# First expert's second row half gathered in three pieces: between the first half's turning and its products, and behind two weight units

## The reference

```python
e_idx = g_star[:, None].astype(jnp.int32) * EXPERTS_PER_GROUP + top_i.astype(jnp.int32)
y = grouped_experts(x, e_idx, w.astype(x.dtype), w_gate, w_up, w_down)

def expert_block(args):
    xblk, e = args
    return (jax.nn.silu(xblk @ w_gate[e]) * (xblk @ w_up[e])) @ w_down[e]
```

## Time and profile before

| | |
|---|---|
| median of 3 runs | 1435.9 us (1434.64 to 1437.3) |
| the profiled execution | 1436.35 us, span 1434.4 us |
| busy: PE, DVE, ACT, POOL | 87%, 30%, 15%, 3% of the span |
| mean granted TensorE clock | 0.947 |
| moved by DMA | 503.63 MB, 351 GB/s over the span |

### The profile page before, as it was taken

How to read it: one execution, slowest core, us unless ns; L and a number is a source line. 1 busy time by engine, 2 the same in 40 slices (tenths; PEclk the granted TensorE clock), 3 DMA queues, 4 the chain that set the end, 5 groups by cost and what they waited for, 6 DMA issues and landing times.

```text
span 1434.4 us, 21171 instructions
## 1 busy us (share of the span) xinstructions
PE 1242.1 (87%) x8998; PEld 675.9 (47%) x8998; DVE 433.2 (30%) x863; ACT 217.4 (15%) x462; POOL 45.4 (3%) x33
## 2 busy tenths in 40 slices
PE   9999999999999998997877778796787787777887
PEld 8888888888788862331222232132232122213223
DVE  4322127674211143322311321231222231132142
ACT  3111232322000043110101111011011010101101
POOL 0000003140000001000000000000000000000000
PEclk9999999999999999998989998899999898999899
DMA  9975443669399359999999999999999999999997
GB/s 342 348 227 183 140 133 121 206 206 340 88 349 413 121 182 427 417 425 435 427 433 432 430 433 431 431 431 431 431 432 432 430 432 432 432 432 430 433 426 317
DMA packets 101202, 503.63 MB, mean 351 GB/s; under 512 B 9294, under 2 KB 79638, under 8 KB 86182
## 3 DMA queue, kind: packets, MB, share of 16 engines
q1 hardware_dynamic: 89346, 494.86, 85.0%
q10 hardware_dynamic: 11812, 8.14, 1.8%
HBM read 496.42 MB, written 6.59 MB: 351 GB/s over the span
## 4 chain that ended last, share of the span: by engine, by line
PE 53%; DMA 44%; DVE 2%; ACT 1%; issue 0%; DVEq 0%; ACTq 0%; SPq 0%
PE bank L735 31%; DMA ring<-in_w_gate 16%; DMA ring<-in_w_up 15%; DMA ring<-in_w_down 12%; PE bank L1023 9%; PE bank L1058 3%; PE bank L958 2%; PE bank L1076 1%; DVE xa L1913 1%; PE bank L1073 1%; DMA xa<-in_x_prompt 1%; PE bank L746 0%; PE bank L826 0%; PE bank L776 0%; PE bank L1084 0%
## 5 line engine op out<-in xcount | busy, mean ns | idle before, releaser
L1023 PE MATMUL bank<-ring,bc 128*32 128x512 f32 x2040 | 272.4, 669 | 113.7 <-DMA ring<-in_w_gate 61.9
L735 PE MATMUL bank<-bc,ring 128*128 128x264 f32 x1536 | 350.8, 387 | 1.3 <-ACT cat L1261 1.3
L735 PEld LDWEIGHTS bank<-bc,ring 128*128 128x128 f32 x1536 | 288.2, 190 | 51.5 <-issue 2.3
L1023 PEld LDWEIGHTS bank<-ring,bc 128*32 128x32 f32 x2040 | 63.7, 118 | 288.2 <-issue 146.5
L1913 DVE TENSOR_TENSOR xa<-xa,bank 128x512 f32<-128x512 f32 x128 | 79.3, 682 | 153.0 <-PE bank L1076 146.6
L735 PE MATMUL bank<-cat,ring 128*128 128x264 f32 x512 | 114.9, 387 | 0.0
L735 PEld LDWEIGHTS bank<-cat,ring 128*128 128x128 f32 x512 | 97.0, 190 | 17.7 <-issue 1.3
L1927 DVE COPY bc<-bank 128x512 f32<-128x512 f32 x32 | 22.1, 691 | 234.6 <-PE bank L1023 234.6
L1058 PE MATMUL bank<-ring,cat 128*32 128x512 f32 x480 | 67.2, 684 | 22.4 <-DMA ring<-in_w_down 22.4
L958 PE MATMUL bank<-cat,bc 128*32 128x512 f32 x512 | 61.3, 597 | 13.5 <-DVE xa L1913 13.5
L1487 ACT ACTIVATE bc<-bank 128x512 f32<-128x512 f32 x32 | 19.1, 597 | 289.6 <-PE bank L1023 289.6
(11 more groups left out here) (300 smaller groups left out, 1023.5 us busy)
## 6 DMA issues: line engine op xcount, KB each, us to landing
ring<-in_w_gate SPq DMA_DIRECT2D x27, 4096.0 KB, 31.8
ring<-in_w_up SPq DMA_DIRECT2D x27, 4096.0 KB, 31.6
ring<-in_w_down SPq DMA_DIRECT2D x26, 4096.0 KB, 32.7
ring<-in_w_in SPq DMA_DIRECT2D x23, 2048.0 KB, 15.3
ring<-in_w_up SPq DMA_DIRECT2D x10, 2048.0 KB, 12.9
ring<-in_w_gate SPq DMA_DIRECT2D x9, 2048.0 KB, 15.4
ring<-in_w_down SPq DMA_DIRECT2D x9, 2048.0 KB, 16.1
ring<-in_w_out SPq DMA_DIRECT2D x8, 2048.0 KB, 16.5
```

The costliest lines, as they stand in the source:

```text
L735: m = pe.matmul(bank[n % 3][:, 0:T], w[:, k, (i % TPU) * P:(i % TPU + 1) * P], src[:, k, :], start=n_k == 0, stop=n_k == KT - 1)
L1023: m = pe.matmul(bank[b][c * C:(c + 1) * C, :], xeT[j % 2][:, k, :], wx, start=i == 0 and x < 4, stop=i == 1 and x >= 4, skip_group_check=True)
```

## The change

`first_rows` takes a list of row tiles, and the turning becomes a function `turn_first`. The first half's rows are gathered as before. Of the second half, the part of prompt tile 0 comes next, then the turning of the first half, then the part of prompt tile 1. The sample part and the turning of the second half stand behind the first expert's g0 and u0. No other engine's code changes.

```diff
-            def first_rows(half):
+            def first_rows(half, ts):
 
-                for t in range(TT):
+                for t in ts:
...
-                m.then_inc(first_gathered, 1)
+                if TT - 1 in ts:
+                    m.then_inc(first_gathered, 1)
 
             keep_busy(6)
-            first_rows(0)
-            first_rows(1)
-            for half in range(2):
+            def turn_first(half):
+
                 pe.wait_ge(first_copied, half + 1)
                 for m_ in (2 * half, 2 * half + 1):
                     m = pe.transpose(bank[(5, 7)[half]][:, m_ * P:(m_ + 1) * P], xrow[:, m_ * P:(m_ + 1) * P], ident)
                 m.then_inc(xe_T, 1)
+
+            first_rows(0, range(TT))
+            first_rows(1, (0,))
+            turn_first(0)
+            first_rows(1, (1,))
...
                         unit_products(j, "g", 0)
                         unit_products(j, "u", 0)
+                        if first:
+                            first_rows(1, (2,))
+                            turn_first(1)
                         pe.wait_ge(xe_ready, 2 * e + 2)
                         unit_products(j, "g", 1)
                         unit_products(j, "u", 1)
```

## The result

The changed kernel takes 1440.47 us in the median of 20 runs (1438.66 to 1444.83), the kernel before 1436.35; the ratio is 1.0027 with a 95% interval of 1.0020 to 1.0034, that is 3.9 us (2.9 to 4.9) slower. One execution of the kernel before took 1607.73 us, and the ratio, which compares fast runs, leaves it out. A second comparison, on another occasion, gives 1.0024 (1.0015 to 1.0033). The profiled execution took 1439.9 us with a span of 1438.1.

The account below looks back on a forecast made before the run. The end was taken to hang on unit 19's issue at 577.06 us, set by TensorE's chain. Terms -1.0 + 1.0 + 1.1 + 1.33 gave +2.4 us, so 1438.3 us, with an 8-in-10 range of 1436.4 to 1440.3.

Parts of the forecast that it names:

- What bounds the kernel: Weight stream last stands still until unit 19's issue at 577.06 us, set by TensorE's chain; the end follows from that.
- Part one: Start of g0: g0 and u0 start 1.0 us sooner, and units 10 and 11 are issued 1.0 us sooner.
- Part two: Second half behind u0: waits of some 0.4 us for its copy and 0.5 for its gain; TensorE alone loses 1.1 us.
- Part three: ScalarE's queue behind the copy, 3.98 us later: fold waits another 1.33 us for the gate copy, starting 2.4 us later.
- the sum: Whole kernel: -1.0 (g0 sooner) + 1.0 (moved work) + 1.1 (copy and gain waits) + 1.33 (fold wait) = +2.4 us.
- Part four: From the fold to unit 19: the shift passes one to one, so unit 19 is issued at 579.5 us.
- the clock rival: TensorE's clock falls at the fold's 1.33 us idle time, adding 1.8: sum 4.2 us, 1440.1 us; 10% chance.
- how the numbers follow: Odds with 0.2% (2.9 us) resolvable: forecast 70%, own range 1437.3 to 1439.5; slower 0.31, same 0.66, faster 0.03.
- The fold does not wait: Rival at the first fold: ScalarE catches up, leaving +1.1 us, 1437.0 us; 8% chance.
- the shift is absorbed: Rival between 544 and 577 us, or at the end: a wait has reserve, nothing reaches 577.06; 1435.9 us, 7%.
- The sooner start is what counts: Rival at 577 us: the stream runs through, so the 1.0 us won at 533 is kept; 1434.9 us, 5%.

Follow-up runs that it names:

- a_defer: Changed kernel with ScalarE's eight sample-row copies moved from ahead of the gate-product copy to behind the first expert's gate matrix; 1438.78 us, ratio 1.0011.
- b_defer: Kernel before with ScalarE's eight sample-row copies moved behind the first expert's gate matrix, as a control; 1436.6 us, ratio 0.9998.
- c_turn: Changed kernel with the sample part back ahead of g0 and only the second half's turning moved, between g0 and u0; 1436.9 us, ratio 1.0000.
- f2_fill: Changed kernel with one 512-column filler product ahead of the first fold and one fewer small product before the gathering; 1440.32 us, ratio 1.0040.
- g2_fill: Kernel before with two 512-column filler products in TensorE's wait near 568 us and two fewer small ones before the gathering; 1436.26 us, ratio 0.9994.
- d_early: Kernel before with two of ScalarE's four prompt tile 0 copies moved ahead of its copy of the first down products; 1434.9 us, ratio 0.9987.
- after_again: The changed kernel once more, unchanged, for a second trace; 1441.6 us, ratio 1.0024.
- h_best: Kernel before with the second half turned between g0 and u0 and ScalarE's prompt tile 0 copies split (c_turn and d_early together); 1435.01 us, ratio 0.9987.
- f_fill: Changed kernel with four small filler products on TensorE ahead of the first fold; 1450.27 us, ratio 1.0098 in four runs.
- g_fill: Kernel before with six small filler products in TensorE's wait near 568 us; 1446.17 us, ratio 1.0068 in five runs.

## Why the prediction was right, and where it was short

**What bounds the kernel** was right, and more exactly than I had claimed. Over nine traces (of the kernel before, the changed one, a_defer, b_defer, c_turn and f2_fill) the span is unit 19's issue plus 857.3 to 857.6 us, while unit 19's issue itself moves over 5 us. g2_fill's 856.4 goes with a tail at full clock. d_early shows the limit of the statement: it holds as long as the stream runs dry.

**Part one** was right: g0 starts 0.99 us sooner behind the gathering (forecast 1.0), and so does unit 10's issue.

**Part two** was 0.1 short. TensorE's own loss is 15.32 - 14.09 = 1.23 us in a_defer, where I had 1.1; the two pauses are 0.50 and 0.52, and the sample part moves at full price (0.63 us in both kernels).

**Part three** was right. ScalarE's copy of the second half slipped by 4.1 us against the gathering (3.98 forecast), its queue kept its 8.3 us, and the fold waited 1.19 us (forecast 1.33). a_defer takes that wait away and gets 1.3 us back, b_defer shows that the copies cost nothing by themselves. The measured structural loss is 2.50 us, the sum said 2.43.

**Part four** was right for the structure: fold to unit 19 is 35.04 us in both kernels. Its words "I take the shift one to one" left out that this stretch has two lengths. Where the clock falls behind the wait near 568 us it takes 36.3 to 36.7.

**The size** was short: 2.4 against 3.9 (2.9 to 4.9), and the slower side of 0.2%, to which I had given three tenths. A difference of 3.9 lies outside of the forecast's own range (1.4 to 3.6 us over 1435.9) and only inside the wide one (0.5 to 4.4), and the median itself, 1440.47, is 0.2 above the top of that, 1440.3; that the wide range held is in part luck. The nearest figure was the clock rival's 4.2, but the one profiled execution of the changed kernel has no fall where that rival put it.

The step that failed is "how the numbers follow": I treated the clock as a rival that is there or not, at 10%, with one place. The traces show it falling now and then at 520 us (in the changed kernel and d_early), near 573 us (in both kernels) and at the fold (in the changed kernel alone), 1.0 to 1.6 us each time. The one profiled execution of the kernel before, on which the sum rests, had none of these. In the three traces of the changed kernel there are one, two and two, in the two of the kernel before none and one. One more fall in the median would be enough for the missing 1.4 us; five traces can't show that it is there. That the changed kernel has more of them because of its idle time at the fold was seen in one trace of three, and f2_fill, whose long runs stay though this idle time is filled, speaks against it as the only source. What makes the changed kernel's long runs stays open.

The 1.8 us in that rival's sum are the 5.34 us of the earlier trace rows, at a granted clock of 0.50, less half of the 7.07 us of the earlier trace rows: one fall at 644 us in the kernel before, where the falls between 515 and 600 us cost 1.0 to 1.6. Against the rival the prediction sets an idle time of 1.81 us that left the clock at 1.00. The trace of after_again shows a fall behind 1.23 us all the same, and the other two of the changed kernel show none behind 1.19 and 1.21.

**The other rivals.** "The fold does not wait" and "the shift is absorbed" are out by the traces. "The sooner start is what counts" is out for this kernel (c_turn), and comes true in the trace of h_best, once unit 19 is early enough: 0.4 us, which the medians do not resolve.

## What to carry to other kernels

Before a wait is moved later on one engine, read what is queued behind it there: here a copy of 0.38 us slipped by 4 us, and took 8 us of unrelated work with it past its reserve of 1.6. Work that hands over from engine to engine (copy, turning, gain) belongs ahead of a unit that can hide each step, not all behind one: here that was two pauses of 0.50 and 0.52 us, and in c_turn none. And in a stream-bound kernel look for the last moment at which the stream runs dry: what moved that moment (66 GB/s at 577 us in the kernel before) moved the end here, up to the point where the stream no longer ran dry, as in d_early (377 GB/s).

## What the runs showed of the hardware that I had not expected

A few more instructions were a cliff here. Four products more in TensorE's straight part raised the packets of instructions from 33 to 88 (0.54 to 1.44 MB, 16 KB each) and cost 11 us in a loop behind them; a filler of like length at an unchanged number of instructions (f2_fill) left the packets at 33 and the end at 857.6 us behind unit 19. The packets and the waits in the loop come together: six waits without a releaser, 37.7 and 37.6 us in all, in the two traces with 88 packets (f_fill, g_fill), and none in the twelve with 33. That the waits are for these packets is inferred from that alone, since the profile does not show when a packet was moved.

The same clock falls in one execution of a kernel and not in the next. Behind the wait of 1.8 us near 568 us (and one of 0.8 us two microseconds later) it fell in five of the ten traces that have both, at a cost of 1.3 to 1.6 us. It fell in none of the four in which the first of the two is gone or filled (d_early, h_best, g_fill, g2_fill); that points to this wait and is too little to prove it. Behind the 1.2 us at the fold it fell in one of three, and behind a wait of 1.3 us at 12 us in one of fourteen (b_defer). At the end all fourteen wait 2.1 us for the last weights: in g2_fill and h_best the last down products run at full clock (PEclk 1.00), 1.92 us for 16 matmuls, and in the others they take 2.8 to 3.5 (PEclk 0.50 from 1413 to 1416 us in the kernel before).
